# Four local changes to a decoder trunk: half-chunk loads at the start, a split order of input sums, one rounding moved from ScalarE to GpSimd, and two-part low halves in the first feed-forward block

## The reference

```python
for i in range(DEPTH):                       # DEPTH = 2
    x = layer_norm(ALPHA*x + 0.5*swiglu(x, ffn1_w_gu[i], ffn1_w_down[i]), ...)
    if i % 2 == 0: y, qm = gla_mix(x @ gla_w_in, ...)      # gated linear attention
    else:          y, qm = conv_mix(x @ conv_w_in, ...)    # depthwise conv, LN, silu
    m = mem_attention(qm, mem, mem_w_kv[i])                # softmax over 256 rows
    x = layer_norm(ALPHA*x + concat([y, m]) @ w_out, ...)
    x = layer_norm(ALPHA*x + 0.5*swiglu(x, ffn2_w_gu[i], ffn2_w_down[i]), ...)
# swiglu: (silu(x @ w_gate) * (x @ w_up)) @ w_down, D_FF = 2816
```

## Time and profile before

| | us |
|---|---|
| median of 3 runs (2047.54 to 2049.7) | 2049.1 |
| the profiled execution | 2050.35 |
| its span | 2048.6 |
| PE busy | 2023.3 |
| DVE busy | 1355.9 |
| ACT busy | 811.7 |
| POOL busy | 786.7 |

### The profile page before, as it was taken

One profiled execution on the slowest core, in us unless ns is written; L12 is line 12 of the kernel. 1 busy time (PEld: TensorE's weight loads), 2 busy tenths in 40 slices (PEclk: granted clock), 3 DMA queues, 4 the chain that ended last, 5 costly groups with the idle time before them and its releaser, 6 DMA issues.

```text
span 2048.6 us, 34293 instructions
## 1 busy us (share of the span) xinstructions
PE 2023.3 (99%) x13509; PEld 1856.2 (91%) x13509; DVE 1355.9 (66%) x1842; ACT 811.7 (40%) x1163; POOL 786.7 (38%) x443
## 2 busy tenths in 40 slices
PE   9999999999999999999999999999999999999998
PEld 9899998988988989999898999989887798999887
DVE  4477774554435768877456877646899886767645
ACT  5433452253423344444234444423353534434422
POOL 1499820033312257881015888001100225877000
PEclk9999999999999999999999999999999999999999
DMA  7545323332211234543232445323544322332232
GB/s 250 185 144 163 123 87 101 101 105 83 63 32 62 93 114 144 164 151 104 99 109 93 161 146 164 105 95 99 185 124 175 103 82 84 102 102 92 89 102 87
DMA packets 229497, 239.13 MB, mean 117 GB/s; under 512 B 5983, under 2 KB 222173, under 8 KB 227612
## 3 DMA queue, kind: packets, MB, share of 16 engines
q1 hardware_dynamic: 228764, 235.68, 35.3%
q10 hardware_dynamic: 640, 2.16, 0.3%
HBM read 215.80 MB, written 22.02 MB: 116 GB/s over the span
## 4 chain that ended last, share of the span: by engine, by line
PE 83%; DVE 5%; POOL 5%; issue 3%; ACT 2%; DMA 1%; DVEq 0%; SPq 0%; ACTq 0%; POOLq 0%
PE bank L1764 11%; PE bank L1766 11%; PE bank L1765 11%; PE bank L1893 10%; PE bank L1894 10%; PE bank L1895 10%; PE bank L1775 4%; PE bank L1776 3%; PE bank L1777 3%; DVE u L1680 2%; POOL xlo L531 1%; ACT whi L662 1%; POOL s L553 1%; POOL diag_tmp L585 1%; PE bank L1799 1%
## 5 line engine op out<-in xcount | busy, mean ns | idle before, releaser
L662 ACT CAST whi<-raw 128x2048 fp32r<-128x2048 f32 (+2 forms) x192 | 325.9, 1699 | 881.6 <-POOL scratch L560 436.4
L1113 DVE TENSOR_TENSOR wlo<-raw,whi 128x2048 fp32r<-128x2048 f32 (+2 forms) x166 | 358.4, 2159 | 243.9 <-ACT whi L662 243.6
L537 POOL TENSOR_TENSOR tiny<-tiny 128x2 f32<-128x2 f32 (+1 forms) x13 | 9.4, 724 | 754.3 <-DVE tiny L1389 754.3
L556 POOL TENSOR_TENSOR raw<-raw 128x512 f32<-128x512 f32 x72 | 220.4, 3062 | 0.0
L1764 PE MATMUL bank<-h_hi,whi 128*128 128x512 f32 x528 | 207.1, 392 | 0.0
L1765 PE MATMUL bank<-h_lo,whi 128*128 128x512 f32 x528 | 205.5, 389 | 0.0
L1766 PE MATMUL bank<-h_hi,wlo 128*128 128x512 f32 x528 | 205.5, 389 | 0.0
L1893 PE MATMUL bank<-t_hi,whi 128*128 128x256 f32 x576 | 163.9, 285 | 2.9 <-DVE bank L1181 2.9
L560 POOL TENSOR_TENSOR scratch<-raw,s 128x512 f32<-128x512 f32 x72 | 149.2, 2072 | 44.2 <-DVE ex_lo L1120 44.2
L1893 PE MATMUL bank<-t_hi,ex_hi 128*128 128x256 f32 x576 | 163.7, 284 | 0.7 <-DVE bank L1173 0.4
L1894 PE MATMUL bank<-xlo,whi 128*128 128x256 f32 x576 | 163.0, 283 | 0.0
(11 more groups left out here) (351 smaller groups left out, 5880.8 us busy)
## 6 DMA issues: line engine op xcount, KB each, us to landing
raw<-in_ffn_w_gu_dram SPq DMA_DIRECT2D x88, 1024.0 KB, 4.9
raw<-in_ffn_w_down_dram SPq DMA_DIRECT2D x32, 896.0 KB, 5.0
raw<-in_ffn_w_down_dram SPq DMA_DIRECT2D x32, 512.0 KB, 3.3
raw<-in_gla_w_in_dram SPq DMA_DIRECT2D x14, 1024.0 KB, 5.1
early_raw<-in_conv_w_in_dram SPq DMA_DIRECT2D x18, 512.0 KB, 4.2
lo_scratch<-early_lo SPq DMA_DIRECT2D x18, 512.0 KB, 3.2
diag_scratch<-diag_tmp SPq DMA_DIRECT2D x8, 1024.0 KB, 8.8
raw<-in_conv_w_in_dram SPq DMA_DIRECT2D x16, 512.0 KB, 5.4
```

Source lines behind the costliest of these rows:

```text
L556: nc.gpsimd.tensor_tensor(a21, a21, a11, ALU.add).then_inc(w_sum, 1)
L662: nc.scalar.copy(whi[:, s, 0:kc, 0:width], raw[:, s, 0:kc, 0:width]).then_inc(hi_ready, 1)
L1113: nc.vector.tensor_tensor(wlo[:, s, 0:kc, 0:width], raw[:, s, 0:kc, 0:width], whi[:, s, 0:kc, 0:width].bitcast(F32), ALU.subtract).then_in ...
```

## The change

1. **Start.** Chunk 1 of the memory weights is loaded, rounded and split in two halves of four blocks each, with semaphores of their own; PE starts it when the first half's low part is there.
2. **x_sums.** All sums wait until x's low parts are complete. Sums 0 and 1 are made ahead of the third chunk's low part, sums 2 and 3 behind it.
3. **Convolution output.** POOL rounds `b_hi_c` in place of ACT. ACT runs one SiLU on a single column earlier, ahead of the scale and offset, and counts `hi_ready` up behind it.
4. **Block 0.** The low part of each chunk of pairs 2 to 10 is made in two operations of four blocks. In the loop the first stands ahead of the fourth combining step, the second behind it and behind the two remainders. Only the second counts `lo_ready`; the first counts `half_ready`, on which PE starts the chunk. PE waits for `lo_ready` ahead of the fourth product. Blocks 1 to 3 keep the single operation.

```diff
@@ SP, start
-            for n in range(1, 8):
+            sp.dma_start(raw[:, 1, 0:4, :], w0[:, 0:4, 256:512]).then_inc(second_loaded, 16)
+            sp.dma_start(raw[:, 1, 4:8, :], w0[:, 4:8, 256:512]).then_inc(raw_loaded[1], 16)
+            for n in range(2, 8):
@@ POOL, convolution output
             split_lo(CONV_OUT_N + 2, 0, B_K, after_dve=True)
-            pool.wait_ge(hi_ready, CONV_OUT_N + 4)
+            pool.wait_ge(raw_loaded[1], 16 * (CONV_OUT_N // 2 + 4))
+            pool.wait_ge(mo_mm, 2 * HEADS)
+            nc.gpsimd.tensor_copy(b_hi_c[:, :, :], raw[:, 1, :, :]).then_inc(b_hi_done, 1)
+            pool.wait_ge(b_hi_done, 1)
             pool.wait_ge(w_used, DIAG_N + len(TAPS_K))
             nc.gpsimd.tensor_tensor(b_lo_c[:, :, :], raw[:, 1, :, :], b_hi_c[:, :, :].bitcast(F32), ALU.subtract).then_inc(lo_ready, 1)
@@ ACT, start
-            split_hi(0, 1)
+            act.wait_ge(second_loaded, 16)
+            nc.scalar.copy(whi[:, 1, 0:4, :], raw[:, 1, 0:4, :]).then_inc(second_hi, 1)
+            act.wait_ge(raw_loaded[1], 16)
+            nc.scalar.copy(whi[:, 1, 4:8, :], raw[:, 1, 4:8, :]).then_inc(hi_ready, 1)
@@ ACT, convolution output
-            act.wait_ge(raw_loaded[1], 16 * (CONV_OUT_N // 2 + 4))
-            act.wait_ge(mo_mm, 2 * HEADS)
-            nc.scalar.copy(b_hi_c[:, :, :], raw[:, 1, :, :]).then_inc(hi_ready, 1)
+            nc.scalar.activation(tiny[:, 68:69], ones[:, 0:1], ACT.Silu)
             affine(LN_CONV, 0, range(DK), c_hi, ROW_CG, ROW_CB, ACT.Silu)
+            act.wait_ge(b_hi_done, 1)
+            act.sem_inc(hi_ready, 1)
@@ DVE, x_sums
-            def x_sums(f):
+            def x_sums(f, js):
                 base = x_base((None, LN_GLA_OUT, LN_FFN[1], LN_CONV_OUT)[f]) if f else 0
-                for j, (to, plus, minus) in enumerate(T_SUM):
-                    if f:
-                        dve.wait_ge(x_hi_ready, base + (DK if j else DK // 2))
-                        dve.wait_ge(x_ready, base + (0, DK // 2, DK, DK)[j])
-                    else:
-                        dve.wait_ge(x_ready, DK)
+                dve.wait_ge(x_ready, base + DK)
+                for j in js:
@@ DVE, plain_pair
                 if i == 0:
-                    x_sums(f)
+                    x_sums(f, (0, 1))
                 else:
                     x_sums_lo(f)
-                split_lo(FFN_N[f] + 2 * i + 2, 0)
+                if f == 0 and i + 1 == PLAIN:
+                    half_lo(FFN_N[f] + 2 * i + 2, 0, 0)
+                    half_lo(FFN_N[f] + 2 * i + 2, 0, 1)
+                else:
+                    split_lo(FFN_N[f] + 2 * i + 2, 0)
+                if i == 0:
+                    x_sums(f, (2, 3))
@@ DVE, new function
+            def half_lo(n, s, part):
+
+                ks = slice(4 * part, 4 * part + 4)
+                dve.wait_ge(hi_ready, n + 1)
+                dve.wait_ge(lo_ready, n)
+                done = nc.vector.tensor_tensor(wlo[:, s, ks, :], raw[:, s, ks, :], whi[:, s, ks, :].bitcast(F32), ALU.subtract)
+                if part:
+                    done.then_inc(lo_ready, 1)
+                else:
+                    done.then_inc(half_ready, 1)
@@ DVE, summed_pair (the up half likewise, with n + 2)
-                split_lo(n + 1, 1)
-                combine(f, i, 0, 3)
-                extra_lo(f, i, 1)
+                if f == 0:
+                    half_lo(n + 1, 1, 0)
+                    combine(f, i, 0, 3)
+                    extra_lo(f, i, 1)
+                    half_lo(n + 1, 1, 1)
+                else:
+                    split_lo(n + 1, 1)
+                    combine(f, i, 0, 3)
+                    extra_lo(f, i, 1)
@@ DVE, start
-            for n in range(1, 10):
+            dve.wait_ge(second_hi, 1)
+            nc.vector.tensor_tensor(wlo[:, 1, 0:4, :], raw[:, 1, 0:4, :], whi[:, 1, 0:4, :].bitcast(F32),
+                                    ALU.subtract).then_inc(second_lo, 1)
+            dve.wait_ge(hi_ready, 2)
+            nc.vector.tensor_tensor(wlo[:, 1, 4:8, :], raw[:, 1, 4:8, :], whi[:, 1, 4:8, :].bitcast(F32),
+                                    ALU.subtract).then_inc(lo_ready, 1)
+            for n in range(2, 10):
@@ PE, seven_products
-                pe.wait_ge(lo_ready, FFN_N[f] + 2 * i + g + 1)
+                if f:
+                    pe.wait_ge(lo_ready, FFN_N[f] + 2 * i + g + 1)
+                else:
+                    pe.wait_ge(half_ready, q + 1)
...
                 product(r6, *weight_sum(1), *x_sum(2)).then_inc(part_mm, 1)
+                pe.wait_ge(lo_ready, FFN_N[f] + 2 * i + g + 1)
                 product(r1, *weight(low, left), *x(low, early))
```

More of the change, by code:

```diff
@@ L318, in build @@
         fin_mm, fin_act, fin_dve, out_stored = (sem(n) for n in ("fin_mm", "fin_act", "fin_dve", "out_stored"))
-        gain_loaded, fin_rows, rows_centred = (sem(n) for n in ("gain_loaded", "fin_rows", "rows_centred"))
+        gain_loaded, fin_rows, rows_centred, b_hi_done = (
+            sem(n) for n in ("gain_loaded", "fin_rows", "rows_centred", "b_hi_done"))
+        half_ready = sem("half_ready")
+        second_loaded, second_hi, second_lo = (sem(n) for n in ("second_loaded", "second_hi", "second_lo"))
         block = ctx.enter_context(nc.Block())
@@ L1123, in extra_lo @@
                                         ALU.subtract).then_inc(ex_lo_ready, 1)
-            def x_sums(f):
+            def x_sums(f, js):
                 base = x_base((None, LN_GLA_OUT, LN_FFN[1], LN_CONV_OUT)[f]) if f else 0
-                for j, (to, plus, minus) in enumerate(T_SUM):
-                    if f:
-                        dve.wait_ge(x_hi_ready, base + (DK if j else DK // 2))
-                        dve.wait_ge(x_ready, base + (0, DK // 2, DK, DK)[j])
-                    else:
-                        dve.wait_ge(x_ready, DK)
+                dve.wait_ge(x_ready, base + DK)
+                for j in js:
+                    to, plus, minus = T_SUM[j]
                     if j:
@@ L1197, in summed_pair @@
                     combine(f, i, 1, step)
-                split_lo(n + 2, 0, DOWN_K[0] if last else 8)
+                if f == 0 and not last:
+                    half_lo(n + 2, 0, 0)
+                else:
+                    split_lo(n + 2, 0, DOWN_K[0] if last else 8)
                 if last:
@@ L1205, in summed_pair @@
                     extra_lo(f, i + 1, 0)
+                    if f == 0:
+                        half_lo(n + 2, 0, 1)
                 dve.wait_ge(w_used, n + 2)
@@ L2135, in _ @@
             for n in range(8):
-                if n:
+                if n >= 2:
                     pe.wait_ge(lo_ready, n + 1)
-                if n >= 2:
                     pe.wait_ge(kv_evac, 2 * (n - 1))
@@ L2147, in _ @@
                                 pe.wait_ge(lo_ready, 1)
+                        elif n == 1 and k == 0:
+                            pe.wait_ge(second_lo, 1)
+                        elif n == 1 and k == 4:
+                            pe.wait_ge(lo_ready, 2)
                         for t in range(2):
```

## The result

| | before | after |
|---|---|---|
| median, us | 2049.4 | 2069.9 |
| runs, us | 2047.5 to 2051.7 | 2068.9 to 2073.1 |
| the profiled execution | 2050.35 | 2070.47 |
| its span | 2048.6 | 2068.7 |

The change makes the kernel slower: the ratio is 1.0102, with a 95% interval of 1.009 to 1.0115. The forecast was 2072.0 us, in a range of 2050 to 2086.

The account below looks back on a forecast made before the run. It took PE, busy for 99% of the span, to bound the kernel. 2050.35 + 0 - 3.9 + 1.9 + 25 = 2073.35, less 1.25 for the median, gave 2072 us, range 2050 to 2086.

Parts of the forecast that it names:

- the list of signs: What would show the forecast: in block 0, PE waits on L1181 and the low halves, POOL idle 3 us or more.
- point (b) of part 4: Block 0: slot's next load issued 5 us or more later; next chunk's combining step 1 queued behind the second half.
- Part 1: Start: PE's wait moves from chunk 1 to chunk 2, effect 0; bounds -1.3 and +1 us.
- Part 2: Blocks 1 to 3: POOL's low parts undisturbed, 1.3 of 1.68 us each, -3.9; bounds -1.95 and -5.0.
- Part 3: Convolution output: front gain given back by late `c_lo`, slow clock behind it, +1.9 us; bounds -4.9 and +4.1.
- The slow clock: Convolution output: PE's new idle is followed by 3 to 4 us at half speed, losing 1.8 us.
- Part 4: Block 0: +25 us; five distances with diagonals 15.5, two without 7, last pair 2, first 0.5; bounds -5.1, +37.
- The round of a slot: Block 0: load, sums, rounding, halves, fourth step and remainders add to 24.4 us; 24.1 taken with diagonals.
- A: Faster: DVE's halves fall into POOL's gaps, load stays hidden, PE's pace of 20.16 rules; 2042 to 2039 us, chance 0.14.
- B: Block 0: shared resource stays the only bound, load hidden, pairs keep 21 us; 2047 us, chance 0.09.
- C: Block 0: only the pairs with a store behind the load suffer; 2063 us, chance 0.12.
- D: Block 0: all turns paid, 26 us a pair, +37 instead of +25; 2084 us, chance 0.13.

Follow-up runs that it names:

- the cut alone: Kernel before with block 0's low part in two operations, both ahead of the fourth combining step; 2060.8 us, ratio 1.0043.
- the late load alone: Kernel before with its single operation, but SP's load in block 0 waits until both remainders are done; 2061.5 us, ratio 1.0045.
- the control: Kernel before with only the first tap's diagonals built and stored, used by the convolution for all four taps; 2045.6 us, ratio 0.9975.
- part 3 alone: Kernel before with only the convolution output change (POOL rounds `b_hi_c`, ACT's early SiLU); 2053.1 us, ratio 1.0015.
- part 4 alone: Kernel before with only the block 0 change (low part in two operations, second behind the remainders); 2074.1 us, ratio 1.0108.
- part 4 without diagonals: The control with the block 0 change on top; 2076.9 us, ratio 1.0127.

## Why the prediction was right

The forecast of 2072.0 was 2 us above the median, and the mechanism was the one given. That it is so near is in part luck: in block 0 terms that were 2.8 and 1.1 us too high stand against one that was 1.3 too low. PE's waits, though, came mostly at the first combining step, and not at the fourth and the low halves, where the list of signs looked for them; point (b) of part 4 names the place. By its steps:

**Part 1: right.** PE stands 1.15 us at 22.20 instead of at 16.36, and starts chunk 2 at the same time as before (22.21). Block 0 starts 0.0 us later.

**Part 2: right mechanism, too small a term.** I took 1.3 of the 1.68 us for a block; all of it came, 1.67 in each of three. The step that failed is "PE needs some of its low parts late even in the undisturbed case": the undisturbed POOL (x8 in 6.23 us) leaves PE only 0.6 us of waits in all. -5.0, the lower bound, in place of -3.9.

**Part 3: +2.3 against +1.9.** The rounding took 1.91 us on POOL, the bound at ACT's price, and not 2.4. The Trainium skill's rule (GPSIMD Engine Reference, section 4.1) had been the better guide here. `c_lo`'s second block, in the time of the kernel before, was ready at 1623.2; I had 1623.6. The slow clock came behind the new stand as forecast. A slip of the sum hides there: 4.57 us of L638 behind 1618.6 end at 1623.2 and not at 1623.0, so `c_lo` should have read 1623.8. What failed is a term that the sum lacks: POOL's next subtraction meeting DVE's last four blocks, the last stand. And 1.9 us as the worth of the slow stretch of before (in the lower bound) was too much: here it costs the stage some 1.2.

**Part 4: +22.4 against +25.** The round of a slot was put at 24.4 and the pair at 24.1; it is 23.55. Term by term, as predicted and in the ring above (starts to starts): load 6.7 and 6.6, four sums 6.7 and 6.5, rounding 2.0 and 2.0, first half 2.5 and 2.2, fourth step 0.4 and 0.3, remainders 3.7 and 3.6, second half 2.4 and 2.3. Every turn was paid, and the sum was 0.85 too long from small roundings up. The five pairs with diagonals gave 12.7 against 15.5. The two without gave 8.3 against 7 (24.7 and 23.9 us, forecast 23.7). There the load (5.0) and the first half (1.22) came as forecast, and the sums, put at about 8, took 6.8. The term that failed is PE, which that ring lacks: DVE waits for PE ahead of the third and again ahead of the fourth step. In the gate slot's round from 261.95 to 285.96, rounding to first half takes 3.35 us instead of 2.0, since ACT is done at 284.5 and DVE still waits for the third step, and first half to fourth step takes 2.54 instead of 1.2:

```profile
285.62 0.43 DVE L1203 SCALAR_TENSOR_TENSOR bank<-bank,p_copy 128x256 f32<-128x256 f32 x1 [1.47 <-PE bank L1937]
285.96 1.22 DVE L1185 TENSOR_TENSOR wlo<-raw,whi 128x1024 fp32r<-128x1024 f32 x1
288.50 0.43 DVE L1206 TENSOR_TENSOR bank<-bank,p_copy 128x256 f32<-128x256 f32 x1 [1.32 <-PE bank L1937]
```

PE, held up at the first combining step, comes later with the products that the later steps take. The first pair gave 1.0 against 0.5, the last 0.4 against 2.

**The rivals.** A (the turns fall into gaps, the load stays hidden) and B fail at POOL's 5.48 us stand. B is shown wrong twice, by the cut alone and the late load alone, which each cost 10 us. C falls with the control. D, every pair at 26, is not reached. The low end of A was miscounted: 2049.1 - 5.1 - 3.9 - 3 is 2037, not 2039; nothing hangs on it.

**Not foreseen:** 0.5 us in the GLA mixer. Most of it, 0.35, comes near 634 us, with a wait of PE of 0.33 us for VectorE's states (L2323) that the kernel before doesn't have; why VectorE is later there stays open. The larger new wait, 1.4 us at L2124, costs nothing: the kernel before has a slow stretch at 449 us that holds PE up by 1.3 us, the changed one has none, and PE then stands for the same operation until the same time. Delays of 0.7 to 0.9 us also stand now and then in blocks 1 and 2, at other pairs in other executions of kernels that are the same there; they are no part of the change, and set how finely milestones of single executions can be compared.

## What to carry to other kernels

Before an instruction is cut or moved behind others, draw the ring that its buffer goes round (load, sums, rounding, remainder, release) and add it up with each engine's turn-taking paid; if the sum is above the pair's length, the ring is the new bound, whatever wait the cut removes. Where two engines take turns by whole instructions, long ones hurt the partner's latency and many short ones hurt its throughput; here no cut brought a gain that could be told from the noise. A change that makes one engine earlier should be followed to what it frees next: in this kernel an earlier ScalarE freed GpSimd's next subtraction into VectorE's last blocks, and that took back part of the gain.

## What the runs showed of the hardware

- GpSimd rounds 128 by 2048 float32 in 1.91 us, ScalarE's time for the same, while its two-input subtraction of this size takes 4.57 undelayed.
- VectorE's operations with one operand in PSUM were not held up beside that rounding: in part 3 alone three of them take 1.87 us, as in the kernel before (1.88). The two-input `c_lo` beside POOL's subtraction took 4.45 in place of 0.68.

```profile
1615.05 1.91 POOL L639 CAST b_hi_c<-raw 128x2048 fp32r<-128x2048 f32 x1
1615.25 1.87 DVE L1434 TENSOR_TENSOR u<-u,bank 128x512 f32<-128x512 f32 x3
1617.04 5.09 POOL L642 TENSOR_TENSOR b_lo_c<-raw,b_hi_c 128x2048 fp32r<-128x2048 f32 x1
1618.24 4.45 DVE L1419 TENSOR_TENSOR c_lo<-u,c_hi 128x512 fp32r<-128x512 f32 x1
```

The Trainium skill, SBUF — State Buffer, section "Who interferes with whom", says just this: a VectorE instruction with two inputs in SBUF contends with a GpSimd instruction that reads SBUF, one with at most one such input, outside VectorE's two-port modes, doesn't. These rows agree.

- The same stand of TensorE is followed by a stretch at a granted clock of 0.50 in one execution and not in another: 3.17 us before the convolution's output product in part 4 alone (clock 1.00) and in part 4 without diagonals (0.50), and 2.20 us twice in block 0, in the changed kernel (1.00) and in part 4 alone (0.50). One such stretch made the stage before the output product 0.3 to 1.2 us longer, two made block 0 2.3 us longer, and one in the GLA mixer cost nothing, because TensorE would have waited behind it anyway. Before a difference of this size between two profiles is put down to the change, the granted clock of both has to be looked at.
